# Attention layer on one core: the second attention half writes three of its four head pairs through DRAM, and its products stand behind the transposes

## The chip, the cores and the metric

The kernel runs on one core of a Trainium2 chip. The metric is the device time of one execution in microseconds (us), the median of several runs.

## What is computed

One decoder layer over 1024 tokens plus 16 meta tokens, width 1024. After a norm and a projection come two attentions of 8 heads each, both of head width 64: a stick-breaking attention, and a softmax attention over at most 256 keys that an indexer selects. Their outputs go through branch weights and sigmoid gates, an output weight, and a squared-ReLU MLP. What matters here is the second attention and what it hands on:

```python
logits = jnp.einsum('bqhd,bqkhd->bhqk', qb, kg) * (D_HEAD ** -0.5)
logits = jnp.where(sel_ok[:, None], logits, -jnp.inf)
p = jax.nn.softmax(logits, axis=-1)
return jnp.einsum('bhqk,bqkhd->bqhd', p, vg)
...
merged = gate_sb * (o_sb @ w_branch_sb) + gate_ds * (o_ds @ w_branch_dsa)
```

## The kernel before

Every fp32 factor is split into a rounded "hi" part and a rest, "lo", and a product is made of hi and lo parts on TensorE (PE). The attention is a list of 128 jobs, JOBS, one for each head and block of 128 queries: jobs 0 to 63 are the stick-breaking heads 0 to 7, jobs 64 to 127 the softmax heads 8 to 15. Within a head the blocks come in the order 7, 0, 6, 1, 5, 2, 4, 3; a block i has 16 + 128 (i + 1) keys, in chunks of at most 512. A loop over steps j, written out by hand for each engine, sets all order. In the second half a step does this:

- PE: scores(j) (L759, L760) into two banks in turn; its first part's products (L810); turn(j - 2), the transposes of the weights of two steps ago (L775); at j % 8 == 4 values(), transposes of the next head's values (L741); at PAIR_AT turn_sums(), transposes of the reciprocal sums of a head pair (L785); then its second part's products.
- ScalarE (ACT): round_weights(j - 2), the cast of the turned weights to pt_hi (L932); at j % 8 == 4 the cast of the values (L941); exponent(j) (L916), which waits for VectorE's logits(j); at RELOAD + 3 the cast of a reloaded pair to o_hi (L967); output(k) of a finished product group; at PAIR_AT the cast of a scaled pair (L963).
- VectorE (DVE): logits(j) (L1163), which frees the score banks; rest_weights(j - 2) (L1192), pt_lo = turned weights - pt_hi; add_bottom (L1206); rest_values (L1200); scale_pair (L1181).
- GpSimd (POOL): the add of a reloaded pair (L681), and the rests o_lo (L684, L688).
- SyncE (SP): the DMA queue, strictly in order.

A product group k = 4 g + n belongs to head g and two of its blocks. Its PSUM result has 128 rows, two parts of 64 that still have to be added. In the first half ACT copies it to o_st (L949), SP writes it to DRAM (`spill`, L599), and later SP loads the two parts of a head pair as o_raw0 and o_raw1 (L648), POOL adds them, ACT rounds them. In the second half ACT copies the upper 64 rows to o_pair (L952) and DVE adds the lower 64 from PSUM (L1206). A group of head g ends in steps 8 g + 6, 8 g + 7, 8 g + 10 and 8 g + 11. Four of SP's steps matter below:

```python
for k in OUT_AT[j]:
    if k < 4 * H:
        spill(k)
if j % NB == 1 and j // NB + 1 < 2 * H:
    ...
    load_head(g)
```

load_head issues six loads of q and k and then two of v_raw. The first half's pairs are reloaded at RELOAD = 70, 80, 90, 100; the first half's last spill stands in step 67.

Of the kernel before, what the change touches and what calls it, by code (L numbers as in the profile page):

```python
# [21 lines left out]
D = 1024  # L22
SEQ = 1024
# [251 lines left out]
def build(nc, x, meta, w_units, b_gate, g_pre, g_post, g_mlp_pre, g_mlp_post, ident, strict, fill,  # L275
          rope_i, rope_d, out):
    with ExitStack() as ctx:
# [9 lines left out]
        def scratch(name, *shape):  # L287
            return nc.dram_tensor(name, shape, F32, kind="Internal").ap()
# [4 lines left out]
        def head_rows(d, half, g):  # L293
# [3 lines left out]
            return d[DS][half].rearrange("(d h) t -> h d t", h=H)[g - H]  # L297
        g_d, o_d = scratch("g_d", 2 * D, SEQ), scratch("o_d", H, 2 * DH, SEQ)
        h1_d = nc.dram_tensor("h1_d", (SEQ, D), F32, kind="Internal").ap()
# [191 lines left out]
        with ExitStack() as st:  # L491
# [44 lines left out]
            def _(sp):  # L536
# [86 lines left out]
                for j in range(NJ + 5):  # L623
                    for u in STARTS[j]:
                        load_unit(sp, u + 2, u % 2)
                    for part in range(2):
                        for n in ENDS[j][part]:
                            store(n)
                    for k in OUT_AT[j]:
                        if k < 4 * H:  # L630
                            spill(k)
                    if j % NB == 1 and j // NB + 1 < 2 * H:
                        g = j // NB + 1
                        for u in HEAD_UNITS[g]:
# [3 lines left out]
                    for p in range(4):  # L638
                        if j == RELOAD[p]:
                            for s in range(2):  # L640
                                sp.wait_ge(o_spilled[s], 16 * 4 * (p + 1))
                            if p == 0:
                                in_dram(U_BRANCH - 1)
                            else:
                                sp.wait_ge(or_lo, p)
                            for half in range(2):
                                for g in range(2):
                                    sp.dma_start(o_raw[half][DH * g:DH * g + DH], o_d[2 * p + g, DH * half:DH * half + DH, :]).then_inc(or_in, 16)  # L648

            @block.gpsimd  # L650
            def _(pool):
# [25 lines left out]
                for j in range(NJ // 2 + 1, NJ + 6):  # L677
                    for p in range(4):
                        if j == RELOAD[p] + 1:
                            pool.wait_ge(or_in, 64 * (p + 1))  # L680
                            pool.tensor_tensor(o_raw[0][:], o_raw[0][:], o_raw[1][:], ALU.add).then_inc(or_sum, 1)  # L681
                        if j == RELOAD[p] + 3:
                            pool.wait_ge(or_hi, p + 1)
                            pool.tensor_tensor(o_lo[:, p, :], o_raw[0][:], o_hi[:, p, :].bitcast(F32), ALU.subtract).then_inc(or_lo, 1)  # L684
                    for p in range(3):
                        if j == PAIR_AT[p]:
# [168 lines left out]
            def _(act):  # L855
# [87 lines left out]
                def output(k):  # L943
                    g = k // 4
                    act.wait_ge(pv_done, k + 1)
                    if g < H:
                        if k >= 2:
                            act.wait_ge(o_spilled[k % 2], 16 * (k // 2))
                        act.copy(o_st[:, k % 2], o_part(k)).then_inc(o_free, 1)  # L949
                    else:  # L950
                        r = DH * (g % 2)
                        act.copy(o_pair[(g - H) // 2][r:r + DH, pair_cols(k)], o_part(k)[0:DH]).then_inc(top_done, 1)  # L952

# [10 lines left out]

                def reload(p):
                    act.wait_ge(or_sum, p + 1)
                    act.copy(o_hi[:, p, :], o_raw[0][:]).then_inc(or_hi, 1)  # L967
# [7 lines left out]
                for j in range(NJ + 5):  # L975
# [12 lines left out]
                    for n in ENDS[j][1]:  # L988
                        evacuate(n)
                    for p in range(4):  # L990
                        if j == RELOAD[p] + 3:
                            reload(p)
                    if j > NJ // 2 and j % 16 == 0:
# [3 lines left out]
                    for p in range(3):  # L997
                        if j == PAIR_AT[p]:
                            round_pair(p)

            @block.vector
            def _(dve):
# [168 lines left out]
                def scale_pair(p):  # L1171
                    if p < 3:
                        dve.wait_ge(o_free, 4 * H + 8 * (p + 1))
                    else:
                        dve.wait_ge(or_lo, 4)
                    for half in range(2):
# [25 lines left out]
                def add_bottom(k):  # L1202
                    g, r = k // 4, DH * (k // 4 % 2)
                    dst = o_pair[(g - H) // 2][r:r + DH, pair_cols(k)]
                    dve.wait_ge(top_done, k + 1 - 4 * H)
                    dve.tensor_tensor(dst, dst, o_part(k)[DH:P], ALU.add).then_inc(o_free, 1)  # L1206
# [18 lines left out]
                for j in range(NJ + 6):  # L1225
                    if 1 <= j < NJ + 1 and JOBS[j - 1][0] == SB:
                        stick(j - 1)
                    if j > NJ // 2 and j % 16 == 0:
                        reciprocals((j - NJ // 2) // 16 - 1)
                    if j < NJ and JOBS[j][0] == DS:  # L1230
                        logits(j)
# [4 lines left out]
                    while spent < due:  # L1236
                        spent += next(search, 1e9)
                    if 2 <= j < NJ + 2:
# [4 lines left out]
                    if j % NB == 4 and j // NB + 1 < 2 * H:  # L1243
                        rest_values(j // NB + 1)
                    if j in PAIR_AT:
                        scale_pair(PAIR_AT.index(j))
                    if j < NJ + 5:
# [1004 lines left out]
```

## Time and profile before

| | us |
|---|---|
| median of 3 runs | 1745.53 |
| the three runs | 1745.53, 1737.97, 1750.38 |
| profiled execution, its time | 1746.8 |
| its span, first to last instruction | 1745.0 |
| second attention half within it | 723.2 to 918.3 |
| mean granted TensorE clock | 0.972 of full speed |

Busy shares of the whole span: PE 94%, weight loads 79%, DVE 71%, ACT 49%, POOL 31%. PE's busy time counts matmuls from start to modelled end, which overlap, so it is an upper bound of its work. A time is a place in the span, counted from its start. A head in the second half is told here by the start of ACT's exponent over 1040 keys, the head's first job: 728.11, 752.15, 773.09, 798.40, 819.45, 844.36, 865.30 and 888.11 for heads 8 to 15.

### The profile page before, as it was taken

To read this page: it belongs to the slowest core of one execution; us is meant where nothing else is said; L and a number is where in the kernel's file an instruction comes from. 1 tells how busy PE (TensorE), PEld (TensorE's weight loads), DVE (VectorE), ACT (ScalarE), POOL (GpSimd) and SP (SyncE) were. 2 spreads that over 40 slices of the span, in tenths; PEclk is the share of its full clock that TensorE was granted. 3 is DMA by queue.
4 is the path that set the end of the run, shared out by engine and by line. 5 is a ranking of instruction groups with operands and counts; after the bars stand their busy time and mean duration, and the time that the engine had idled before them with its cause. 6 is when DMAs were issued, how large, how long until landed. Compare 5 with 4: busy or idle time off the path is not lost. (4 is left out here: it accounts for less than half of the span.)

```text
span 1745.0 us, 23454 instructions
## 1 busy us (share of the span) xinstructions
PE 1638.4 (94%) x8360; PEld 1384.4 (79%) x8360; DVE 1245.4 (71%) x1966; ACT 851.5 (49%) x1650; POOL 539.7 (31%) x332
## 2 busy tenths in 40 slices
PE   4999899999999999889889999989999999999997
PEld 4889888799877777777777878768888878888885
DVE  5287798888988989687873435785454548777878
ACT  5266555555445545576751133555555543333334
POOL 1111254555434435321102450475545510000000
PEclk6999999999999999998989999999999999999999
DMA  4564434344233233355304443243444365443434
GB/s 172 155 194 124 128 120 134 108 137 114 89 106 107 92 106 107 91 134 135 86 1 163 139 169 121 72 158 133 145 149 174 136 229 217 157 159 131 169 138 103
DMA packets 101372, 231.23 MB, mean 133 GB/s; under 512 B 11192, under 2 KB 25848, under 8 KB 101256
## 3 DMA queue, kind: packets, MB, share of 16 engines
q1 hardware_dynamic: 100680, 227.64, 40.7%
q0 software_dynamic: 576, 2.10, 0.7%
q8 instruction: 67, 1.10, 0.3%
q14 instruction: 49, 0.40, 0.1%
HBM read 155.83 MB, written 73.86 MB: 132 GB/s over the span
## 5 line engine op out<-in xcount | busy, mean ns | idle before, releaser
L710 PE MATMUL bk<-x_hi,w_hi 128*128 128x512 f32 (+2 forms) x832 | 308.7, 371 | 1.2 <-PEq L353 1.2
L710 PE MATMUL bk<-x_lo,w_hi 128*128 128x512 f32 (+2 forms) x832 | 299.3, 360 | 0.0
L710 PE MATMUL bk<-x_hi,w_lo 128*128 128x512 f32 (+2 forms) x832 | 298.5, 359 | 0.0
L666 POOL TENSOR_TENSOR pt_lo<-a_buf,pt_hi 128x512 fp32r<-128x512 f32 (+3 forms) x104 | 138.4, 1347 | 193.0 <-ACT pt_hi L930 192.8
L334 POOL TENSOR_TENSOR w_lo<-w_raw,w_hi 128x1024 fp32r<-128x1024 f32 x53 | 130.4, 2460 | 190.9 <-ACT w_hi L330 190.7
L1087 DVE TENSOR_SCALAR_CACHE_REDUCE counted<-sc,small 128x272 uint8<-128x272 f32 (+6 forms) x217 | 182.5, 891 | 0.9
L1674 PE MATMUL bank<-v_hi,f_hi 128*128 128x512 f32 x448 | 174.3, 389 | 0.0
L1674 PE MATMUL bank<-v_hi,f_lo 128*128 128x512 f32 x448 | 174.3, 389 | 0.0
L1674 PE MATMUL bank<-v_lo,f_hi 128*128 128x512 f32 x448 | 174.3, 389 | 0.0
L710 PEld LDWEIGHTS bk<-x_hi,w_lo 128*128 128x128 f32 x832 | 158.5, 191 | 17.6
L710 PEld LDWEIGHTS bk<-x_hi,w_hi 128*128 128x128 f32 x832 | 159.1, 191 | 16.1 <-issue 1.3
L710 PEld LDWEIGHTS bk<-x_lo,w_hi 128*128 128x128 f32 x832 | 158.8, 191 | 13.3
L810 PE MATMUL bk<-pt_hi,v_hl 128*128 128x256 f32 (+2 forms) x384 | 115.2, 323 | 10.6 <-ACT o_st L949 5.7
L1542 POOL TENSOR_TENSOR s_lo<-s,s_hi 128x512 fp32r<-128x512 f32 x64 | 95.2, 1491 | 72.9 <-ACT s_hi L1718 72.9
L1192 DVE TENSOR_TENSOR pt_lo<-bk,pt_hi 128x512 fp32r<-128x512 f32 (+2 forms) x120 | 62.4, 553 | 74.3 <-ACT pt_hi L932 73.0
L929 ACT COPY a_buf<-bk 128x512 f32<-128x512 f32 (+3 forms) x104 | 54.3, 522 | 107.4 <-PE bk L775 107.4
L1542 POOL TENSOR_TENSOR s_lo<-u_raw,s_hi 128x512 fp32r<-128x512 f32 x48 | 67.9, 1419 | 123.9 <-ACT s_hi L1718 123.9
L775 PE MATMUL bk<-idf,a_buf 128*128 128x128 f32 (+1 forms) x704 | 101.0, 278 | 4.1 <-DVE pt_lo L1192 2.5
L1143 DVE TENSOR_TENSOR_SCAN n_buf<-n_buf 128x1040 f32<-128x1040 f32 (+3 forms) x64 | 101.9, 1591 | 2.3 <-ACT n_buf L906 2.3
L810 PEld LDWEIGHTS bk<-pt_hi,v_hl 128*128 128x128 f32 (+1 forms) x384 | 76.9, 200 | 32.4 <-issue 14.6
L759 PE MATMUL bk<-k_hi,q_st 128*128 128x348 f32 (+6 forms) x224 | 80.1, 361 | 22.9 <-ACT n_buf L906 11.6
L1651 PE MATMUL bank<-m_hi,s_hi 128*128 128x512 f32 x256 | 99.9, 390 | 1.1 <-DVE m_lo L1939 1.1
(228 smaller groups left out, 3861.0 us busy)
## 6 DMA issues: line engine op xcount, KB each, us to landing
w_raw<-w_units SPq DMA_DIRECT2D x57, 512.0 KB, 3.7
f_raw<-f_d SPq DMA_DIRECT2D x28, 1024.0 KB, 5.0
u_raw<-w_units SPq DMA_DIRECT2D x32, 512.0 KB, 4.8
f_d<-f_s SPq DMA_DIRECT2D x64, 256.0 KB, 2.2
b<-w_units SPq DMA_DIRECT2D x16, 1024.0 KB, 8.3
f_d<-c SPq DMA_DIRECT2D x48, 256.0 KB, 2.1
k_hi<-k_d SPq DMA_DIRECT2D x32, 260.0 KB, 5.6
k_lo<-k_d SPq DMA_DIRECT2D x32, 260.0 KB, 6.1
```

Source lines behind the costliest of these rows:

```text
L334: pool.tensor_tensor(w_lo[:, s], w_raw[:, s], w_hi[:, s].bitcast(F32), ALU.subtract).then_inc(lo_done, 1)
L666: pool.tensor_tensor(pt_of(pt_lo, j, tiles), raw, pt_of(pt_hi, j, tiles).bitcast(F32), ALU.subtract).then_inc(sb_lo, 1)
L710: mm = pe.matmul(pj[b][:, 0:c1 - c0], w[:, s, kt, :], a[:, kt, c0:c1], start=kt == 0 and k == 0, stop=kt == KT - 1 and k == 2)
L759: pe.matmul(dst, q, k_hi[s][:, c0:c1], start=True, stop=False)
L775: mm = pe.transpose(bk[TP_BANK[n]][0:r, m * P:(m + 1) * P], a_buf[:, j % 3, col:col + r], idf[:])
L810: mm = pe.matmul(dst, v_hl[0:r, g % 2, slot, :], w[0:r, cols], start=slot == 0 and w is hi, stop=slot == o + 1 and w is lo)
L1087: op(dve.tensor_scalar(counted[:, blk(b)], sc[:, blk(b)], cand[:, j:j + 1], None, ALU.is_ge, ALU.add, accum_out=cnt[:, j:j + 1]))
L1143: dve.tensor_tensor_scan(n[:, ::-1], n[:, ::-1], n[:, ::-1], 1.0, ALU.mult, ALU.bypass).then_inc(scan_done, 1)
L1192: dve.tensor_tensor(pt_of(pt_lo, j, tiles), bk[TP_BANK[n]][:, 0:m * P].rearrange("p (c k) -> p c k", c=m), pt_of(pt_hi, j, tiles).bitcast( ...
L1542: pool.tensor_tensor(s_lo[k % RING][:], first_raw(*FIRST[k]), s_hi[k % RING][:].bitcast(F32), ALU.subtract).then_inc(s_lo_done, 1)
L1651: mm = pe.matmul(dst, w[r][:, n, :], b, start=p in (1, 2, 5) and n == 0 and i == 0, stop=n == HT - 1 and i == 2, skip_group_check=True)
L1674: mm = pe.matmul(dst, a[r][:, q, t * P:(t + 1) * P], w[r][:, q, :], start=p in (1, 5, 2) and q == 0 and n == 0, stop=q == QP - 1 and n == ...
```

## The change

The second half's three first head pairs (heads 8 to 13, groups 32 to 55) are treated as the first half's: ACT copies all 128 rows to o_st, SP spills them, and three more reloads bring them back, the one part into o_pair, the other into o_raw1; POOL adds them and DVE's scale_pair waits for that. Only heads 14 and 15 keep the old way. The seven reloads stand at steps 70, 78, 85, 90, 95, 101 and 117. From step 66 PE runs all products of a step behind the transposes. DVE's rest_weights moves from the end of a step to the start of the next, and rest_values and scale_pair one step on; PAIR_AT moves four steps on.

```diff
+SECOND_HALF = NJ // 2 + 2
-RELOAD = [NJ // 2 + 6 + 10 * p_ for p_ in range(4)]
-PAIR_AT = [NJ // 2 + 16 * (p_ + 1) + 4 for p_ in range(3)] + [NJ + 1]
+RELOAD = [(NJ // 2 + step_, p_) for step_, p_ in ((6, 0), (14, 1), (21, 4), (26, 2), (31, 3), (37, 5), (53, 6))]
+PAIR_AT = [NJ // 2 + 16 * (p_ + 1) + 8 for p_ in range(3)] + [NJ + 1]
+K_LAST = 4 * H + 24
@@ SP
-                        if k < 4 * H:
+                        if k < K_LAST:
                             spill(k)
-                        if j == RELOAD[p]:
+                        if j == step:
                             for s in range(2):
                                 sp.wait_ge(o_spilled[s], 16 * 4 * (p + 1))
-                            if p == 0:
+                            if n == 0:
                                 in_dram(U_BRANCH - 1)
                             else:
+                                sp.wait_ge(or_sum, n)
+                            if 1 <= p < 4:
                                 sp.wait_ge(or_lo, p)
@@ POOL
+                        if j == step + 1:
+                            whole = o_raw[0] if p < 4 else o_pair[p - 4]
+                            pool.wait_ge(or_in, 64 * (n + 1))
+                            pool.tensor_tensor(whole[:], whole[:], o_raw[1][:], ALU.add).then_inc(or_sum, 1)
@@ PE
-                    for k, slots in PRODUCTS[j][0]:
-                        product(k, slots)
+                    if j < SECOND_HALF:
+                        for k, slots in PRODUCTS[j][0]:
+                            product(k, slots)
...
+                    if j >= SECOND_HALF:
+                        for k, slots in PRODUCTS[j][0]:
+                            product(k, slots)
@@ ACT
-                    if g < H:
+                    if k < K_LAST:
                         if k >= 2:
                             act.wait_ge(o_spilled[k % 2], 16 * (k // 2))
                         act.copy(o_st[:, k % 2], o_part(k)).then_inc(o_free, 1)
...
-                        if j == RELOAD[p] + 3:
-                            reload(p)
+                        if j == step + 3 and p < 4:
+                            reload(n, p)
@@ DVE
+                    if j > SECOND_HALF and j - 3 < NJ:
+                        rest_weights(j - 3)
...
-                        if k >= 4 * H:
+                        if k >= K_LAST:
                             add_bottom(k)
```

PE in a step whose first part has products (the third step of head 15; pt_hi and pt_lo are the weights, a_buf what is turned), before:

```order
L759 MATMUL bk<-k_hi_352,q_st_350 128x456 [waits f_zdused]
L760 MATMUL bk<-k_lo_354,q_st_350 128x456
L759 MATMUL bk<-k_hi_352,q_st_350 128x456 [waits f_zdused]
L760 MATMUL bk<-k_lo_354,q_st_350 128x456
L810 MATMUL bk<-pt_hi_359,v_hl 128x256 [waits f_tpfree]
L810 MATMUL bk<-pt_lo_361,v_hl 128x256
```

and the same place in the change:

```order
L764 MATMUL bk<-k_hi_352,q_st_350 128x456 [waits f_zdused]
L765 MATMUL bk<-k_lo_354,q_st_350 128x456
L764 MATMUL bk<-k_hi_352,q_st_350 128x456 [waits f_zdused]
L765 MATMUL bk<-k_lo_354,q_st_350 128x456
L780 MATMUL bk<-idf,a_buf 16x128 [waits f_tpfree,f_exp]
L780 MATMUL bk<-idf,a_buf 128x128 x3
L780 MATMUL bk<-idf,a_buf 128x128 [waits f_tpfree]
L780 MATMUL bk<-idf,a_buf 128x128 x3
L780 MATMUL bk<-idf,a_buf 128x128 [waits f_tpfree]
L815 MATMUL bk<-pt_hi_359,v_hl 128x256 [waits f_tpfree]
L815 MATMUL bk<-pt_lo_361,v_hl 128x256
```

The transposes (L775, now L780) moved ahead of the products (L810, now L815).

SP around the third reload of a first-half pair (step 90), before: the loads of head 12 and at once the reload.

```order
L594 DMA v_raw<-v_d 64x528
L595 DMA v_raw<-v_d 64x512
L648 DMA o_raw_347<-o_d 64x1024 [waits f_orlo,f_ospill1,f_ospill0]
L648 DMA o_raw_347<-o_d 64x1024
```

In the change:

```order
L601 DMA o_d<-o_st 128x256 [waits f_ofree] x2
L593 DMA q_st_349<-q_d 64x1024 [waits f_stored0,f_stored1,f_z,f_tp]
L594 DMA k_hi_351<-k_d 64x1040
L595 DMA k_lo_353<-k_d 64x1040
L593 DMA q_st_349<-q_d 64x1024
L594 DMA k_hi_351<-k_d 64x1040
L595 DMA k_lo_353<-k_d 64x1040
L596 DMA v_raw<-v_d 64x528
L597 DMA v_raw<-v_d 64x512
L601 DMA o_d<-o_st 128x256 [waits f_ofree]
L652 DMA o_raw_347<-o_d 64x1024 [waits f_orsum,f_orlo,f_ospill1,f_ospill0]
```

Spills now stand ahead of the head's loads and between them and the reload, and each waits for ACT's copy of that step (f_ofree).

DVE where a head begins (L1163, now L1172, are logits; 128x144 is the head's second job), before:

```order
L1192 TENSOR_TENSOR pt_lo_361<-bk,pt_hi_359 128x4x128 [waits f_tphi]
L1192 TENSOR_TENSOR pt_lo_361<-bk,pt_hi_359 128x2x128 [waits f_tphi]
L1206 TENSOR_TENSOR o_pair_366<-o_pair_366,bk 64x256 [waits f_top]
L1163 ISA n_buf,small<-bk,small 128x144 [waits f_z,f_exp]
L1163 ISA small 128x1
```

and in the change:

```order
L1202 TENSOR_TENSOR pt_lo_361<-bk,pt_hi_359 128x4x128 [waits f_tphi]
L1202 TENSOR_TENSOR pt_lo_361<-bk,pt_hi_359 128x2x128 [waits f_tphi]
L1172 ISA n_buf,small<-bk,small 128x144 [waits f_z,f_exp]
L1172 ISA small 128x1
```

Only the add left; rests and logits stand in the order in which they stood.

## Rows read from the trace of the kernel before

**Rows 1.** Windows of the second half, and heads 9, 10, 13, 14.

```profile
core 0: us, PE busy (x) PEld busy (x) DVE busy (x) ACT busy (x) POOL busy (x), PEclk, DMA share, GB/s
723.20:918.30 195.10, 166.19 (x1088) 140.45 (x1087) 141.93 (x394) 130.91 (x311) 32.06 (x16) 0.91 0.41 93
752.15:773.09 20.94, 18.03 (x131) 15.07 (x129) 17.31 (x50) 15.36 (x38) 4.77 (x2) 1.00 0.64 143
773.09:798.40 25.31, 21.90 (x139) 18.55 (x137) 18.39 (x51) 17.15 (x41) 4.74 (x2) 0.87 0.32 71
844.36:865.30 20.94, 18.04 (x131) 15.07 (x129) 17.29 (x50) 14.39 (x38) 0.51 (x1) 1.00 0.43 93
865.30:888.11 22.81, 19.31 (x136) 16.21 (x135) 18.21 (x51) 16.16 (x39) 2.38 (x1) 0.97 0.18 38
```

**Rows 2.** Waits in head 13: total us, times, longest.

```profile
ACT pt_hi L932 <- PE bk L775: 5.1, 4, 2.0
DVE pt_lo L1192 <- ACT pt_hi L932: 2.5, 5, 1.0
...
PE bk L759 <- DVE small L1163: 1.5, 1, 1.5
...
PE bk L775 <- DVE pt_lo L1192: 0.8, 1, 0.8
PE bk L810 <- issue: 0.5, 1, 0.5
```

**Rows 3.** Timeline of head 13, third step: last product, turn, cast, rest.

```profile
847.60 0.28 PE L810 MATMUL bk<-pt_lo,v_hl 128*128 128x128 f32 x1
...
847.72 1.15 PE L775 MATMUL bk<-idf,a_buf 128*16 128x128 f32 x9
...
848.97 0.69 DVE L1192 TENSOR_TENSOR pt_lo<-bk,pt_hi 128x512 fp32r<-128x512 f32 x1 [0.52 <-ACT pt_hi L932]
```

**Rows 4.** Timeline of head 13, seventh step: first product, turn, rest.

```profile
857.01 0.28 PE L810 MATMUL bk<-pt_hi,v_hl 128*128 128x256 f32 x1
...
857.90 0.93 PE L775 MATMUL bk<-idf,a_buf 128*16 128x128 f32 x7
...
859.15 0.69 DVE L1192 TENSOR_TENSOR pt_lo<-bk,pt_hi 128x512 fp32r<-128x512 f32 x1 [1.01 <-ACT pt_hi L932]
```

**Rows 5.** DVE's adds, by line, from 720 to 925.

```profile
L1206 DVE TENSOR_TENSOR o_pair<-o_pair,bk 64x256 f32<-64x256 f32 x32 | 13.6, 424 | 5.8 <-ACT o_pair L952 4.9
```

**Rows 6.** Timeline: one spill; head 14's loads, ACT's output before them, values() in head 13.

```profile
724.72 0.32 SPq L599 DMA_DIRECT2D o_d<-o_st  x1
...
838.83 0.44 SPq L591 DMA_DIRECT2D q_st<-q_d  x1
...
842.32 0.36 ACT L952 COPY o_pair<-bk 64x256 f32<-64x256 f32 x1
...
842.51 0.60 SPq L594 DMA_DIRECT2D v_raw<-v_d  x1
843.15 0.60 SPq L595 DMA_DIRECT2D v_raw<-v_d  x1
...
852.37 0.53 PE L741 MATMUL bk<-idf,v_raw 64*16 64x64 f32 x9
```

**Rows 7.** DMA issues from 720 to 920: KB each, median us to landing.

```profile
v_raw<-v_d SPq DMA_DIRECT2D x7, 128.0 KB, 6.4
```

**Rows 8.** Timeline: a reload that nothing else overlaps, and POOL's add of it.

```profile
757.96 2.36 SPq L648 DMA_DIRECT2D o_raw<-o_d  x4
...
765.05 2.39 POOL L681 TENSOR_TENSOR o_raw<-o_raw,o_raw 128x1024 f32<-128x1024 f32 x1 [7.19 <-DMA o_raw<-o_d]
```

**Rows 9.** ACT: output and, three steps on, the cast's place, for steps 70, 78, 90.

```profile
747.38 0.36 ACT L952 COPY o_pair<-bk 64x256 f32<-64x256 f32 x1
...
754.34 1.06 ACT L967 CAST o_hi<-o_raw 128x1024 fp32r<-128x1024 f32 x1
...
768.18 0.36 ACT L952 COPY o_pair<-bk 64x256 f32<-64x256 f32 x1
...
775.82 0.44 ACT L916 ACTIVATE a_buf<-n_buf,small 128x144 f32<-128x144 f32 x1
...
804.57 0.36 ACT L952 COPY o_pair<-bk 64x256 f32<-64x256 f32 x1
...
811.26 1.03 ACT L967 CAST o_hi<-o_raw 128x1024 fp32r<-128x1024 f32 x1
```

**Rows 10.** Window with the granted clock in head 10.

```profile
786.00:790.00 4.00, 4.00 (x17) 3.54 (x16) 1.77 (x5) 2.04 (x4) 2.37 (x1) 0.50 0.02 4
```

More of the change, by code:

```diff
@@ L637, in _ @@
                         load_head(g)
-                    for p in range(4):
-                        if j == RELOAD[p]:
+                    for n, (step, p) in enumerate(RELOAD):
+                        if j == step:
                             for s in range(2):
                                 sp.wait_ge(o_spilled[s], 16 * 4 * (p + 1))
-                            if p == 0:
+                            if n == 0:
                                 in_dram(U_BRANCH - 1)
                             else:
+                                sp.wait_ge(or_sum, n)
+                            if 1 <= p < 4:
                                 sp.wait_ge(or_lo, p)
-                            for half in range(2):
+                            for half, dst in enumerate((o_raw[0] if p < 4 else o_pair[p - 4], o_raw[1])):
                                 for g in range(2):
-                                    sp.dma_start(o_raw[half][DH * g:DH * g + DH], o_d[2 * p + g, DH * half:DH * half + DH, :]).then_inc(or_in, 16)
+                                    sp.dma_start(dst[DH * g:DH * g + DH], o_d[2 * p + g, DH * half:DH * half + DH, :]).then_inc(or_in, 16)
             @block.gpsimd
@@ L677, in _ @@
                 for j in range(NJ // 2 + 1, NJ + 6):
[L678 to L681, printed above, removed]
-                        if j == RELOAD[p] + 3:
+                    for n, (step, p) in enumerate(RELOAD):
+                        if j == step + 1:
[3 more added lines that the diff above has]
+                        if j == step + 3 and p < 4:
                             pool.wait_ge(or_hi, p + 1)
@@ L951, in output @@
                         r = DH * (g % 2)
-                        act.copy(o_pair[(g - H) // 2][r:r + DH, pair_cols(k)], o_part(k)[0:DH]).then_inc(top_done, 1)
+                        act.copy(o_pair[3][r:r + DH, pair_cols(k)], o_part(k)[0:DH]).then_inc(top_done, 1)
                 def spread(p):
@@ L963, in round_pair, with reload @@
                     act.copy(o_hi[:, 4 + p, :], o_pair[p][:]).then_inc(op_hi, 1)
-                def reload(p):
-                    act.wait_ge(or_sum, p + 1)
+                def reload(n, p):
+                    act.wait_ge(or_sum, n + 1)
                     act.copy(o_hi[:, p, :], o_raw[0][:]).then_inc(or_hi, 1)
@@ L989, in _ @@
                         evacuate(n)
-                    for p in range(4):
-                        if j == RELOAD[p] + 3:
-                            reload(p)
+                    for n, (step, p) in enumerate(RELOAD):
+                        if j == step + 3 and p < 4:
+                            reload(n, p)
                     if j > NJ // 2 and j % 16 == 0:
@@ L1172, in scale_pair @@
                     if p < 3:
-                        dve.wait_ge(o_free, 4 * H + 8 * (p + 1))
+                        dve.wait_ge(or_sum, [q for _, q in RELOAD].index(4 + p) + 1)
                     else:
+                        dve.wait_ge(or_sum, len(RELOAD))
                         dve.wait_ge(or_lo, 4)
@@ L1237, in _ @@
                         spent += next(search, 1e9)
-                    if 2 <= j < NJ + 2:
+                    if 2 <= j < SECOND_HALF:
                         rest_weights(j - 2)
                     for k in (OUT_AT[j - 1] if j else ()):
-                        if k >= 4 * H:
+                        if k >= K_LAST:
                             add_bottom(k)
[L1243 to L1246, printed above, removed]
+                    late = int(j > SECOND_HALF)
+                    if (j - late) % NB == 4 and (j - late) // NB + 1 < 2 * H:
+                        rest_values((j - late) // NB + 1)
+                    if j - late in PAIR_AT:
+                        scale_pair(PAIR_AT.index(j - late))
                     if j < NJ + 5:
```

12 lines of the change are left out of this document (6 added, 6 removed).

## The prediction

> **What bounds the kernel now.** I read the windows first. The second attention half takes 195.1 us of the 1745.0 [rows 1]; nothing outside it is touched, so all that follows is a sum over its eight heads. An undisturbed head (9 or 13) takes 20.94 us at full clock, and in it PE is busy 18.0 us, DVE 17.3 and ACT 14.4 to 15.4 [rows 1]. So three engines are nearly full at once, PE most of all. PE idles 2.9 us in such a head, and the waits say where [rows 2]: 1.5 us once, when the third chunk of the head's first scores waits for DVE's logits; 0.8 us once, when a transpose waits for a bank that DVE's rest has to free; 0.5 us once ahead of a product. No change of order alone can give more than these 2.9 us a head. DVE itself waits 2.5 us for ACT's casts, and ACT 5.1 us for PE's transposes [rows 2]: the ring PE transpose, ACT cast, DVE rest, DVE logits, PE scores goes around, and products stand inside it.
>
> Heads 10 and 14, in which a pair's sums are turned and scaled, take 25.31 and 22.81 us [rows 1]. The second is nearly all at full clock (0.97) and so shows the price of the pair, 22.8 - 20.9 = 1.9 us. The first ran at 0.87; its extra 2.5 us is the price of one stretch at half clock, 1.2 GHz [rows 10]. The mean clock of the half is 0.91 [rows 1].
>
> **The change part by part: what it gives.** (a) DVE loses 24 of the 32 adds at 0.424 us [rows 5], 10.2 us of work, four adds (1.7 us) in each of six heads; ACT's copy of 128 rows in place of 64 has the same columns and I cost it at nothing. (b) On PE the transposes go ahead of the products of the first part. In the third step of head 13 DVE waits 0.52 us for the cast behind the transpose at 847.72, which starts when the products end [rows 3]; in the seventh step the products take 857.90 - 857.01 = 0.9 us and DVE waits 1.01 us behind them [rows 4]. Both waits go. (c) DVE's rests change their place in the code but not in its sequence, so that edit alone is worth nothing.
>
> What does PE get of this? Between the seventh step and the next head's scores DVE wins the wait of 1.0, one add of 0.4 and some 0.2 of smaller gaps: 1.6 us, and the scores' wait of 1.5 us is covered by it. The product's 0.5 shrinks to 0.3 with it. The bank's 0.8 stays, since between step 2 and step 5 PE, ACT and DVE are all packed and products only change places with transposes. That is 1.7 us a head for heads 8 to 13. In heads 14 and 15 the adds remain and I take 1.0. Sum 6 x 1.7 + 2 x 1.0 = 12.2 us. (d) turn_sums leaves the step in which it shares four banks with two groups of weights and two of values. PE's eight transposes and DVE's two multiplies remain. I take half of the 1.9 us, 0.9 for each of three pairs: 2.8. Together 15 us are given.
>
> **What it costs.** (e) The spills tie SP to ACT. Until now SP ran ahead in this half: head 14's loads were issued from 838.83, and v_raw's two loads at 842.51 and 843.15 [rows 6], landing 6.4 us after issue [rows 7], at 849.6, well ahead of values() at 852.37. Now the spill of the head's last step stands ahead of load_head and waits for ACT's output, which ended at 842.32 + 0.36 = 842.68. With 0.3 for the spill's issue the loads start at 843.0, v_raw's second follows 843.15 - 838.83 = 4.3 later, and lands at 843.0 + 4.3 + 6.4 = 853.7. That is 1.3 us too late at the old pace, and 2.0 with the quicker head. PE already waits 0.8 us right behind (the bank), so some 1.2 are left. Six heads (9 to 14) are concerned; in 9, 10 and 12 the next item comes before it and hides it. 3 x 1.2, less what head 11 shares with its reload: 3 us.
>
> (f) The reloads. A reload is issued at step j, and ACT takes its sum at step j + 3, whatever SP did. Before, SP ran ahead and ACT never waited. Now reloads 70, 78, 90 and 95 stand directly behind a spill of the same step, so behind ACT's output of that step. From there: 0.3 for the spill's issue [rows 6], 765.05 - 757.96 = 7.1 from the first issue to landing, and 2.4 for POOL's add [rows 8]: the sum is there 9.8 us after the output ended. ACT reaches its cast after 754.34 - 747.74 = 6.6 us (step 70), 776.26 - 768.54 = 7.7 (step 78), 811.26 - 804.93 = 6.3 (step 90) [rows 9]. ACT would stand 3.2, 2.1 and 3.5 us. For step 95, which is followed by a head's long first jobs but whose reload also waits for POOL's previous rest, I estimate 1.5 (between 0 and 3.5, the ends of the others). Behind the waiting ACT stand the casts of the next weights; DVE waits for them with its next logits, and PE can run ahead only by two score banks. Lower bound of the cost: nothing, if ACT, 73% busy, catches up. Upper: all of it. After each of these places ACT, PE and DVE are packed for four steps (there ACT has no slack to give), so I take all: 10.3 us.
>
> For (f) the Trainium skill says otherwise: "DMA: Bandwidth & Descriptors", section "Anatomy of one DMA — SWDGE (gpsimd) path", fits a DMA as 2.0 us plus its bytes at 436 GB/s. Taken for the 1 MB of a reload as a whole, my estimate by that page is 4.4 us; ACT's stands would shrink to some 0.5, 0, 0.8 and 0, and the kernel would come out near 1736. The row of this trace has 7.1 us with POOL idle and waiting for it, for DMAs of SP's queue, so the sum goes by the row.
>
> (g) Three more reloads (85, 101, 117) feed DVE's scale_pair. From the last spill of a pair to that step lie six steps, some 15 us at 2.6 a step; the way is 0.3, the spill's landing (which I take at 2, between nothing and v_raw's 6.4), 7.1 and 2.4, some 12 us and at most 16.2. Covered, or nearly. POOL's adds, 7 us, are hidden: it is busy 4.8 of 21 us in a head [rows 1].
>
> Sum: 3 + 10.3 = 13.3 us of cost against 15.0 given, so 1.7 less: 1746.8 - 1.7 = 1745.1. The profiled execution is 1.3 above the median of the runs, which is inside their spread of 12 us. **Forecast: 1745 us**, no change that can be told; about 1% (17 us) is what a measurement of this kernel can tell from none.
>
> **The rivals.** *The stands are hidden.* If ACT's waits fall into idle time (it waits 5.1 us a head for PE anyway [rows 2]) or the reloads land sooner, only (e) is left: -15 + 3 = -12. A denser PE may also lose one or two of the half-clock stretches at 2.5 each: -14.5 to -17, so 1730 to 1735. For it: DVE, not ACT, is the engine PE waits for. Against it: in the packed steps every cast is followed at once by someone's wait. Chance 0.27. Of it 0.05 is for the shorter transfer by the fit of the Trainium skill.
>
> *The stands bring half clock, and it is slower.* Place: the four waits of ACT and three of v_raw. A stand of 2 to 3.5 us leaves PE without work, longer than the 1.5 us that it waits now. If five of seven stands open one more stretch at 2.5 us, that is 12.5; with all of (e) and (f) at the quicker pace (0.6 more on each of the seven, 4) the sum is -15 + 13.3 + 4 + 12.5 = +15: 1762. It decides from about three extra stretches. For it: the clock fell in head 10 (0.87) with no stand at all. Against it: head 13 has its wait of 1.5 us and stayed at 1.00 [rows 1, 2]. Chance 0.18.
>
> *The order does nothing.* PE is at 18 of 20.9 us, and products behind transposes may delay the next scores by what the transposes gain. Then 5 us are given, and at the slower pace the costs are 9: 1751. Chance 0.07.
>
> The forecast itself, 1738 to 1752, has 0.48.
>
> **How the numbers follow.** The range leaves out half of the best end of the first rival and the upper half of the second: 1730 to 1760. Faster by over 1% (under 1729) needs the first rival and both clock gains: 0.14. Slower by over 1% (over 1763) is the far half of the second: 0.12. The rest, 0.74, is within.
>
> **What would show it.** In the changed profile: an undisturbed head (13 after the change) 19 to 20.5 us; no wait of L759's successor for logits over 0.5 us; ACT's cast of o_hi from o_raw waiting for POOL's add three or four times, 1.5 to 4 us each (this is the step I am least sure of); PE's transposes of v_raw waiting for a DMA, 1 to 2 us, in three to six heads; scale_pair not waiting for POOL; the mean clock of the half near 0.91. If those waits of ACT are absent, (f) is wrong and the time lies near 1733; if they are there and the heads are still short, ACT had the slack that I deny it.

## The result: slower by 1.0%, and the profile after

| | before | after |
|---|---|---|
| median of 4 runs each | 1741.97 us | 1759.67 us |
| lowest and highest | 1737.97, 1750.38 | 1756.43, 1764.86 |
| profiled execution: time, span | 1746.8, 1745.0 | 1758.25, 1756.1 |
| second half in it | 723.2 to 918.3 | 724.3 to 930.9 |

The ratio is 1.0104, with the interval 1.0059 to 1.0149: 17.7 us slower. The second run of the changed kernel, inside the experiments below, gave 1.0092 [1.0070, 1.0114]. The profiled executions are 11.5 us apart in time, and 11.5 us lie in the second half: 206.6 us in place of 195.1. That is less than 17.7 because runs of one kernel spread by 8 to 12 us, and the profiled execution of before was a long one, 4.8 us above its median, while that of the change lies 1.4 below its own. Waits and places can be compared between the two profiles; a difference of a few us in total time or a few hundredths of mean clock can't.

The windows of the changed kernel, for the half and for heads 9, 10, 12, 13 and 14, and one stretch in head 12:

```profile
core 0: us, PE busy (x) PEld busy (x) DVE busy (x) ACT busy (x) POOL busy (x), PEclk, DMA share, GB/s
724.30:930.90 206.60, 171.19 (x1088) 143.04 (x1086) 129.85 (x370) 129.31 (x311) 39.12 (x19) 0.89 0.50 118
754.51:780.09 25.58, 20.00 (x128) 16.68 (x127) 15.54 (x46) 15.08 (x39) 4.73 (x2) 0.90 0.66 150
780.09:802.28 22.19, 19.24 (x134) 15.93 (x133) 15.12 (x45) 15.91 (x39) 7.09 (x3) 0.96 0.75 172
828.67:856.15 27.48, 22.72 (x134) 19.05 (x133) 15.03 (x45) 15.92 (x39) 7.11 (x3) 0.80 0.63 147
856.15:878.62 22.47, 19.32 (x136) 16.15 (x135) 16.52 (x48) 15.07 (x38) 2.38 (x1) 0.97 0.48 114
878.62:901.79 23.17, 21.06 (x134) 17.39 (x134) 15.78 (x46) 14.87 (x39) 2.36 (x1) 0.88 0.56 131
842.00:850.00 8.00, 8.00 (x35) 7.04 (x33) 2.85 (x9) 2.73 (x7) 1.01 (x1) 0.50 0.54 131
```

Beside [rows 1], DVE has lost its 24 adds (394 to 370 instructions, 141.93 to 129.85 us busy) and POOL has gained 7 us, both as meant. Still none of heads 8 to 14 is shorter than before's undisturbed 20.94. Head 9 grew by 4.6 us. Heads 10 and 14, which no longer turn a pair's sums (that is now in heads 11, 13 and 15), take 22.19 and 23.17 us. The last row is a stretch of 8 us at half clock within head 12. Head 12 was not free of half clock before: it ran at 0.50 from 820.00 to 825.00, at its start. Its mean clock was 0.89, as this row of before shows, and is 0.80 now:

```profile
819.45:844.36 24.91, 21.68 (x142) 18.39 (x140) 18.39 (x51) 17.11 (x41) 6.59 (x3) 0.89 0.51 114
```

The waits from 720 to 960, the same columns as [rows 2], of which these rows matter:

```profile
DVE pt_lo L1202 <- ACT pt_hi L941: 46.0, 38, 4.9
...
ACT pt_hi L941 <- PE bk L815: 36.1, 14, 5.6
...
PE bk L764 <- DVE small L1172: 18.3, 22, 4.0
...
ACT pt_hi L941 <- PE bk L780: 15.2, 12, 2.9
...
ACT o_hi L976 <- POOL o_raw L686: 10.8, 3, 4.9
...
PE bk L746 <- DMA v_raw<-v_d: 6.6, 4, 3.8
...
DVE small L1178 <- ACT a_buf L925: 3.1, 4, 0.9
```

The same view of before, over the same stretch:

```profile
ACT pt_hi L932 <- PE bk L775: 43.3, 32, 3.9
...
DVE pt_lo L1192 <- ACT pt_hi L932: 29.1, 39, 3.2
...
PE bk L759 <- DVE small L1163: 11.1, 9, 1.6
...
ACT o_hi L963 <- DVE o_pair L1181: 6.8, 3, 2.5
```

Four of the rows shown are new after the change: ACT's cast of the weights waits for products (L815), ACT's o_hi for POOL, PE for v_raw, DVE's reciprocal for ACT. The first is the largest, and the prediction doesn't name it. Its 36.1 us are not a loss of 36.1: the cast's wait for transposes fell from 43.3 to 15.2 at the same time, so ACT's waits for PE before this cast grew by 8.0 in all. What such a row costs is read from the times of the experiments. DVE's wait for the casts grew by 16.9 us, PE's wait for logits by 7.2. One wait went: ACT no longer stands for DVE's scaled pair (6.8 us).

Where that first wait is from shows in the timeline of head 13. Its third step, which answers to [rows 3]:

```profile
859.58 1.14 PE L780 MATMUL bk<-idf,a_buf 128*16 128x128 f32 x9
...
860.48 0.36 PE L815 MATMUL bk<-pt_hi,v_hl 128*128 128x256 f32 x1
...
861.10 0.28 PE L815 MATMUL bk<-pt_lo,v_hl 128*128 128x128 f32 x1
...
861.46 1.07 ACT L941 CAST pt_hi<-bk 128x512 fp32r<-128x512 f32 x2 [1.87 <-PE bk L815]
...
862.08 0.69 DVE L1202 TENSOR_TENSOR pt_lo<-bk,pt_hi 128x512 fp32r<-128x512 f32 x1 [1.12 <-ACT pt_hi L941]
```

And its seventh, which answers to [rows 4]:

```profile
869.76 0.93 PE L780 MATMUL bk<-idf,a_buf 128*16 128x128 f32 x7
...
870.44 0.36 PE L815 MATMUL bk<-pt_hi,v_hl 128*128 128x256 f32 x1
...
871.66 0.97 ACT L941 CAST pt_hi<-bk 128x512 fp32r<-128x512 f32 x2 [2.21 <-PE bk L815]
...
872.28 0.69 DVE L1202 TENSOR_TENSOR pt_lo<-bk,pt_hi 128x512 fp32r<-128x512 f32 x1 [1.29 <-ACT pt_hi L941]
```

The transposes start ahead of the products, as planned, but the cast behind them starts 1.9 us after they do, and only when the last product has ended. pt_hi and pt_lo have two buffers, one for each product group in turn, and round_weights holds one more wait:

```python
if k == 0 and pair_of(j) >= 2:
    act.wait_ge(pv_done, pair_of(j) - 1)
```

The weights turned in the third and the seventh step go into the buffer from which the products of that same step read. While the products stood first, that wait was met when the transposes ended: in the waits of before, the cast waits for L775 only, never for L810. Now transposes and products run one after the other before the cast may start. DVE's waits of 0.52 us [rows 3] and 1.01 us [rows 4] became 1.12 and 1.29.

The reload of step 70 in the timeline, and the casts of the next and of the fifth reload:

```profile
750.54 0.37 ACT L958 COPY o_st<-bk 128x256 f32<-128x256 f32 x1
...
750.94 0.32 SPq L601 DMA_DIRECT2D o_d<-o_st  x1
...
751.42 2.37 SPq L652 DMA_DIRECT2D o_raw<-o_d  x4
...
758.76 2.37 POOL L686 TENSOR_TENSOR o_raw<-o_raw,o_raw 128x1024 f32<-128x1024 f32 x1 [25.60 <-DMA o_raw<-o_d]
...
761.16 1.05 ACT L976 CAST o_hi<-o_raw 128x1024 fp32r<-128x1024 f32 x1 [4.34 <-POOL o_raw L686]
...
784.92 1.05 ACT L976 CAST o_hi<-o_raw 128x1024 fp32r<-128x1024 f32 x1 [1.57 <-POOL o_raw L686]
...
820.20 1.04 ACT L976 CAST o_hi<-o_raw 128x1024 fp32r<-128x1024 f32 x1 [4.89 <-POOL o_raw L686]
...
821.77 1.16 DVE L1202 TENSOR_TENSOR pt_lo<-bk,pt_hi 128x512 fp32r<-128x512 f32 x2 [4.92 <-ACT pt_hi L941]
```

From the end of ACT's output (750.91) to the sum (761.13) it is 10.2 us. ACT stands, and in the last two rows DVE stands just as long behind it. The values' loads, in heads 12 and 13:

```profile
841.37 0.76 PE L746 MATMUL bk<-idf,v_raw 64*16 64x64 f32 x9 [3.78 <-DMA v_raw<-v_d]
...
854.04 0.35 ACT L958 COPY o_st<-bk 128x256 f32<-128x256 f32 x1
...
854.41 0.33 SPq L601 DMA_DIRECT2D o_d<-o_st  x1
...
855.39 0.45 SPq L593 DMA_DIRECT2D q_st<-q_d  x1
...
859.73 0.59 SPq L597 DMA_DIRECT2D v_raw<-v_d  x1
```

Head 14's loads start 0.8 us before head 13 does (856.15); before, they started 5.5 us before it (838.83 and 844.36). SP waits for ACT. The longest wait, 3.78 us in head 12, is for loads that stood behind the fifth reload as well, and PE's 8 us at half clock follow it directly. These loads also took 7.8 to 8.2 us to land, where the median in this half is 6.5.

### The profile page after: what moved, and what is told of

Read it like the earlier page. It is cut to its first block and busy times, and to the rows that moved or that the text cites. A ratio compares the mean times of both kernels' runs of the same rounds, so it can differ in the third digit from the quotient of the medians.

```text
span 1756.1 us, 23499 instructions
## 1 busy us (share of the span) xinstructions
PE 1644.8 (94%) x8360; PEld 1388.2 (79%) x8360; DVE 1230.6 (70%) x1942; ACT 850.0 (48%) x1650; POOL 550.0 (31%) x335
## 5 line engine op out<-in xcount | busy, mean ns | idle before, releaser
L815 PE MATMUL bk<-pt_hi,v_hl 128*128 128x256 f32 (+2 forms) x384 | 115.0, 323 | 9.6 <-ACT o_st L958 6.1
L780 PE MATMUL bk<-idf,a_buf 128*128 128x128 f32 (+1 forms) x704 | 105.7, 287 | 3.2 <-DVE pt_lo L1202 1.6
L1572 POOL DMA_DIRECT2D out<-scaled x4 | 3.6, 897 | 314.8 <-DVE scaled L2150 314.8
```

The lines of the kernel that those rows point to most:

```text
L780: mm = pe.transpose(bk[TP_BANK[n]][0:r, m * P:(m + 1) * P], a_buf[:, j % 3, col:col + r], idf[:])
L815: mm = pe.matmul(dst, v_hl[0:r, g % 2, slot, :], w[0:r, cols], start=slot == 0 and w is hi, stop=slot == o + 1 and w is lo)
```

## Experiments

Ratios are to the kernel before, run beside it on the same chip, with 95% intervals; 1% is 17.4 us. A ratio uses all runs, so it can differ from the quotient of the two medians by up to 0.001. Prices in us are worked out from the ratios. Where two changed kernels are compared, both intervals count: a difference under some 0.003, 5 us, is not clear of noise.

**The order alone.** The kernel before, with only PE's order of the change:

```diff
-                    for k, slots in PRODUCTS[j][0]:
-                        product(k, slots)
+                    if j < NJ // 2 + 2:
+                        for k, slots in PRODUCTS[j][0]:
+                            product(k, slots)
...
+                    if j >= NJ // 2 + 2:
+                        for k, slots in PRODUCTS[j][0]:
+                            product(k, slots)
                     for k, slots in PRODUCTS[j][1]:
```

> The kernel before with only PE's order changed: from step 66 the products of the first part stand behind the transposes. Theory (the cast waits for the products): 4 to 8 us slower than before, 1.002 to 1.005, with ACT's cast waiting some 30 us in all for products, and DVE's wait in the third step of a head 1.1 in place of 0.5 us. Rival 1 (the order is neutral): within 1 us of before. Rival 2 (the order gives what the prediction took, about 1 us a head): 6 to 10 us faster.

Measured: 1747.95 us, 1.0035 [1.0021, 1.0049], so 6.1 us slower. Its waits, and its head 13 in the third step:

```profile
ACT pt_hi L936 <- PE bk L810: 29.1, 20, 2.8
```

```profile
849.11 1.25 ACT L936 CAST pt_hi<-bk 128x512 fp32r<-128x512 f32 x3 [2.27 <-PE bk L810]
...
849.73 1.49 DVE L1196 TENSOR_TENSOR pt_lo<-bk,pt_hi 128x512 fp32r<-128x512 f32 x3 [1.12 <-ACT pt_hi L936]
```

With nothing spilled, the wait for products is there, in the place and with the DVE wait of 1.12 us that the changed kernel has. The order costs; it doesn't give. The cast's waits for PE add up to 43.0 us here (29.1 for products, 13.9 for transposes) against 43.3 before, so the 6.1 us come not from a longer sum of waits but from where they stand.

**The order undone.** The changed kernel with the products first again:

```diff
-                    if j < SECOND_HALF:
-                        for k, slots in PRODUCTS[j][0]:
-                            product(k, slots)
+                    for k, slots in PRODUCTS[j][0]:
+                        product(k, slots)
...
-                    if j >= SECOND_HALF:
-                        for k, slots in PRODUCTS[j][0]:
-                            product(k, slots)
```

> The changed kernel with PE's order undone: products of the first part ahead of the transposes again, all else as changed. Theory (the order itself costs, since ACT's cast may not overwrite pt_hi before the products of the same step have read it, so with products last the cast waits for transposes and products one after the other): the wait of ACT's cast for products (36 us in all) goes, a head gets 0.6 to 1.2 us shorter, the kernel 5 to 9 us faster than the changed one, 1.005 to 1.008 of the kernel before; the stands of ACT for the reloads and of PE for v_raw stay or grow. Rival (the order is neutral or gives something, all of the loss is stands): no faster than the changed kernel, 1.009 to 1.013.

Measured: 1748.85 us, 1.0048 [1.0029, 1.0066]. That is 8 to 10 us better than the change (1.0092 and 1.0104), a little more than the 5 to 9 expected. ACT's waits for POOL (10.8 us) and PE's for v_raw (8.5 us) stay.

**The casts later.** The changed kernel, ACT's cast of a reloaded pair and POOL's rest of it at the reload's step + 5 in place of + 3:

```diff
-                        if j == step + 3 and p < 4:
+                        if j == step + 5 and p < 4:
```

> The changed kernel with ACT's cast and POOL's rest of a reloaded pair five steps behind the issue in place of three. Theory (ACT's stands of 4.3, 1.6 and 4.9 us cost in full): ACT no longer waits for POOL's add, 8 to 10 us faster than the changed kernel, less 2 us since the reload of step 95 must wait longer for POOL: 1.004 to 1.007 of before. Rival (ACT had the slack): at most 3 us faster than the changed kernel, 1.009 to 1.011.

Measured: 1759.39 us, 1.0109 [1.0093, 1.0124]: no gain at all, and the expectation missed. ACT's stand for POOL is gone, but two other waits grew from 36.1 and 6.6 us:

```profile
ACT pt_hi L941 <- PE bk L815: 47.0, 17, 5.3
...
PE bk L746 <- DMA v_raw<-v_d: 12.9, 5, 7.1
```

The waits for v_raw have two origins. In head 9 (first row of the changed kernel, second of this run) the loads were issued at the same place in both, but while ACT stood 4.34 us, v_raw had time to land; without that stand PE arrives earlier and waits:

```profile
767.34 0.76 PE L746 MATMUL bk<-idf,v_raw 64*16 64x64 f32 x9
...
767.00 0.76 PE L746 MATMUL bk<-idf,v_raw 64*16 64x64 f32 x9 [3.89 <-DMA v_raw<-v_d]
```

In head 12 the wait grew from 3.78 to 7.12 us, and there PE does not arrive earlier: it starts to wait at 837.42, against 837.59 in the changed kernel. The values land later, since the edit itself delays SP. The fifth reload must wait until POOL's rest of the pair before it is done (`or_lo`), and that rest now stands two steps later. The reload moves from 825.54 to 828.22, and head 13's loads stand behind it:

```profile
825.54 2.56 SPq L652 DMA_DIRECT2D o_raw<-o_d  x4
...
SPq L649 <- POOL o_lo L689: 1.8, 1, 1.8
...
828.22 2.37 SPq L652 DMA_DIRECT2D o_raw<-o_d  x4
...
844.54 0.76 PE L746 MATMUL bk<-idf,v_raw 64*16 64x64 f32 x9 [7.12 <-DMA v_raw<-v_d]
```

So this run doesn't price ACT's stands alone. The kernels below that cast later also move the fifth reload behind head 13's loads.

**The values first.** The changed kernel, the two loads of v_raw ahead of the six of q and k:

```diff
@@ load_head
+                    sp.dma_start(v_raw[0:DH, :], v_d[g * DH:(g + 1) * DH, 0:T // 2 + 8]).then_inc(v_in, 16)
+                    sp.dma_start(v_raw[DH:P, 0:T // 2 - 8], v_d[g * DH:(g + 1) * DH, T // 2 + 8:T]).then_inc(v_in, 16)
...
-                    sp.dma_start(v_raw[0:DH, :], v_d[g * DH:(g + 1) * DH, 0:T // 2 + 8]).then_inc(v_in, 16)
-                    sp.dma_start(v_raw[DH:P, 0:T // 2 - 8], v_d[g * DH:(g + 1) * DH, T // 2 + 8:T]).then_inc(v_in, 16)
```

> The changed kernel with load_head's two loads of v_raw ahead of the six of q and k. Theory (PE's four waits for v_raw, 6.6 us in all, cost most of their length): the waits go, 4 to 6 us faster than the changed kernel, 1.006 to 1.009 of before. Rival (PE gets the time back as the ring of DVE and ACT is what is late): within 2 us of the changed kernel, 1.009 to 1.012.

Measured: 1749.20 us, 1.0048 [1.0031, 1.0066]. The waits for v_raw are gone. The gain is 8 to 10 us, where 4 to 6 were expected and the waits add up to 6.6; the intervals leave some 5 us on either side, so that it is more than their length is likely and not shown.

**All three.** Products first, casts at + 5 with the fifth reload two steps later (at 33 for 31), values first:

> The changed kernel with three edits together: products ahead of the transposes again, the casts of the reloaded pairs five steps behind the issue (and the fifth reload at step 97, behind the loads of head 13, in place of 95), v_raw loaded first. What is left of the change is the way through DRAM. Theory (order, stands of ACT and stands for v_raw are all of the loss, and what is saved on DVE is worth something once they are gone): no wait for v_raw, none of ACT for POOL, faster than before by 3 to 10 us, 0.994 to 0.998. Rival (PE and its half-clock stretches set the time, DVE's adds are worth nothing): 0.999 to 1.001.

Measured: 1737.89 us, 0.9973 [0.9956, 0.9989]. The way through DRAM can pay. Not every stand is gone: ACT waits once, 2.4 us, for POOL's add of a reloaded pair, and DVE and ACT now wait for the moved pairs (below).

**The same with the order of the change**, so that the order is priced where no stand hides it:

> The same as the kernel with all three edits, but with the change's order on PE (products behind the transposes). Theory (both stands gone, the order's 6 us remain): 1.000 to 1.003, 5 to 8 us behind the kernel with all three. In the run with the cast alone moved, the stand only changed its place from ACT to PE's wait for v_raw (12.9 us); here neither is left. Rival (the cast is useless also with v_raw first): 1.004 to 1.006, as with v_raw first alone.

Measured: 1745.79 us, 1.0022 [1.0004, 1.0039]. Against the kernel just above, run beside it, the order costs 0.0049, 8.5 us, clear of noise.

**The casts kept.** Products and values first, the casts left at + 3 and the fifth reload at 31:

> The changed kernel with products ahead of the transposes again and v_raw first, but ACT's casts of the reloaded pairs left three steps behind the issue. Against the kernel with all three edits (0.9973) it prices ACT's stands alone, where no later wait for v_raw can take their place. Theory (the stands, some 11 us in three places, cost most of their length): ACT waits 10 to 11 us for POOL's add, 1.001 to 1.004 of before, 6 to 11 us slower than with all three edits. Rival (ACT has the slack, as the run with the cast alone moved could be read): 0.997 to 0.999.

Measured: 1742.63 us, 1.0011 [1.0000, 1.0021], 0.0038 or 6.6 us behind the kernel with all three. Its stands for POOL:

```profile
ACT o_hi L972 <- POOL o_raw L686: 11.1, 3, 5.5
```

The kernel with all three has 2.4 us of these, so 8.7 us fewer, and in turn 3.9 us of DVE's waits for POOL, which this one lacks. The 6.6 us are the price of the early casts and the earlier fifth reload together; the stands cost a good part of their length, and how much exactly stays open.

**SP tied to ACT, no transfers.** The kernel before, where SP waits at the places of the 24 new spills, but moves nothing:

```diff
                         if k < 4 * H:
                             spill(k)
+                        elif k < 4 * H + 24:
+                            sp.wait_ge(top_done, k + 1 - 4 * H)
```

> The kernel before, its way of the second half kept, with nothing but a wait in SP where the change has a spill: for each of groups 32 to 55 SP waits for ACT's copy of that group. Theory (the tie of SP to ACT costs, not the transfers): ACT stands some 3 us before its casts in steps 73 and 93, PE waits 1 to 2 us for v_raw in three to five heads, 1.003 to 1.007. Rival (the added transfers or their landing cost, the tie does not): 0.999 to 1.001.

Measured: 1752.32 us, 1.0063 [1.0040, 1.0086], 11 us slower, with both kinds of new wait:

```profile
ACT o_hi L969 <- POOL o_raw L683: 5.5, 2, 3.1
...
PE bk L743 <- DMA v_raw<-v_d: 3.2, 3, 2.0
```

Stands of both kinds thus come from the tie alone, with none of the new traffic there. They are smaller than in the changed kernel (10.8 and 6.6 us); of the four reloads, which stand at steps 70, 80, 90 and 100 here, only those at 70 and 90 share their step with the end of a group. What makes up the rest in the changed kernel, the later and denser reloads or the transfers, was not separated.

**DVE's adds left out.** The kernel before without the adds of groups 32 to 55. The lower part of heads 8 to 13 is not added in; ACT's copy then frees the bank:

```diff
-                        act.copy(o_pair[...][r:r + DH, pair_cols(k)], o_part(k)[0:DH]).then_inc(top_done, 1)
+                        act.copy(o_pair[...][r:r + DH, pair_cols(k)], o_part(k)[0:DH]).then_inc(o_free if k < 4 * H + 24 else top_done, 1)
...
-                        if k >= 4 * H:
+                        if k >= 4 * H + 24:
                             add_bottom(k)
```

> The kernel before without DVE's adds of groups 32 to 55: the lower 64 rows of heads 8 to 13 are left out of the result, nothing else changes. It prices term (a) of the prediction alone, 10.2 us of DVE's work. Theory (DVE stands in the ring with PE, some 0.5 us a head come out): 3 to 6 us faster, 0.997 to 0.998. The prediction's own figure for heads without adds, with the order: 1.7 us a head, 0.994. Rival (PE sets the time): 0.999 to 1.001.

Measured: 1729.21 us, 0.9931 [0.9911, 0.9951], 12.0 us faster for 10.2 us of DVE's work, where 3 to 6 were expected: a miss. The edit also lets ACT's copy free the bank in place of DVE's add, as the change does; before has no wait of PE for an add in this half. Windows of the half and of head 13:

```profile
core 0: us, PE busy (x) PEld busy (x) DVE busy (x) ACT busy (x) POOL busy (x), PEclk, DMA share, GB/s
723.20:901.22 178.02, 154.93 (x1089) 131.42 (x1088) 129.43 (x371) 130.98 (x311) 32.07 (x16) 0.97 0.44 101
835.11:854.67 19.56, 17.81 (x131) 15.07 (x129) 15.27 (x46) 14.31 (x37) 1.14 (x1) 1.00 0.44 97
```

An undisturbed head takes 19.56 us against 20.94 [rows 1], 1.4 less for 1.7 of adds, with both at full clock; over six heads that is 8.3 us. The half's mean clock is 0.97 against 0.91, but these profiled executions lie 2.6 us below the median (this run) and 5.7 above it (before), so the pair overstates the difference. Over all runs the mean clock of the whole program is 0.986 without the adds (6 runs) and 0.980 before (23 runs): the same direction, and smaller.

**The reciprocals.** The kernel with all three, and DVE's reciprocals of a pair's sums behind rest_weights again, where they stood before the change:

```diff
-                    if j > NJ // 2 and j % 16 == 0:
-                        reciprocals((j - NJ // 2) // 16 - 1)
...
+                    if j > NJ // 2 and j % 16 == 0:
+                        reciprocals((j - NJ // 2) // 16 - 1)
```

> The kernel with all three edits, and DVE's reciprocals of a pair behind the step's rest of the weights in place of ahead of it, as in the kernel before. Theory (ahead of the rests DVE waits 0.9 us for ACT's exponent, 3.1 us in four places, and PE's scores wait for DVE there): the wait goes, 1 to 3 us faster than with all three edits, 0.995 to 0.997 of before. Rival (the wait only takes the place of another): the same as with all three edits, 0.997.

Measured: 1732.50 us, 0.9954 [0.9931, 0.9978]: 8.0 us faster than the kernel before with the whole computation, and the fastest such kernel here. DVE's wait for the exponent is gone. Against the kernel with all three it is 3.3 us faster (0.9973 and 0.9954, each against its own runs of before); the intervals overlap, so this step is not clear of noise.

**The pair's sums later still.** That kernel with PAIR_AT + 11 for + 8:

> The same, and the sums of a pair turned and scaled three steps later still (steps 91, 107 and 123 in place of 88, 104 and 120), so that the pair's reload has three steps more to arrive. Theory (DVE's waits of 3.9 us in two places for POOL's add of a reloaded pair, longest 2.9, cost their length): these waits go, 2 to 4 us faster than the one without this edit, 0.993 to 0.996 of before. Rival (the pair's work costs the same wherever it stands): no difference, 0.995 to 0.997.

Measured: 1738.69 us, 0.9974 [0.9958, 0.9989]. By 3.5 us slower than the kernel above, where I expected faster; the two intervals overlap, so at least the gain of 2 to 4 us isn't there. DVE's waits for POOL's add are gone as meant, but its waits for ACT's casts rose from 27.7 to 32.4 us.

**The change again**, word for word, beside the two kernels above:

> The changed kernel once more, word for word, on the same chip as the two beside it, to set the steps between the kernels against one another: 1.009 to 1.012 of before, by both theories.

Measured: 1757.19 us, 1.0092 [1.0070, 1.0114].

## Why the prediction was wrong

The forecast was 1745, no change; 17.7 us were lost. The measured 1759.67 lies just inside the range of 1730 to 1760 only because the sum started from the profiled 1746.8, 4.8 above the median of before. In differences, 1.7 us of gain were predicted and 17.7 us of loss came. The experiments form a chain from before to after: the adds left out, -12.0; the adds done through DRAM and POOL, with the pairs moved and everything spaced well, +4.0 (0.9954 against 0.9931); the reciprocals moved, +3.3 (0.9973 against 0.9954); the order, +8.5; the values' loads last, the casts early and the fifth reload two steps sooner, +12 to +14 (1.0022 to 1.0092 or 1.0104). The sum is +16 to +18, and must be, since each link starts where the last one ends; the +4.0 and the +3.3 are not clear of noise, the others are.

Beside the prediction's sum this says where it went wrong. The costs (e) and (f), put at 13.3 together, measured 12 to 14. The gains, put at 15.0, measured a loss of about 4: 12.0 from the adds, less 8.5 for the order, 3.3 for the reciprocals and 4.0 for the way through DRAM with the moved pairs.

**The step that failed is (b)**, "on PE the transposes go ahead of the products", with its "Both waits go". They became longer, since ACT's cast of those weights needs the buffer that the products still read. The part of the 12.2 us that was to come from it, some 8 us, came out as a cost of 6.1 us alone and of 8 to 10 in the changed kernel. That the releaser is the buffer is read from the traces and the code; a third pair of buffers, which would prove it, was not tried.

(a), DVE's adds, gave all that (a) and (b) together were to give: 12.0 us measured, 12.2 predicted. That the two numbers agree is luck. In the prediction, 1.0 of the 1.7 us a head is (b)'s wait, and of four adds one counts. So the order was to bring 8 us (8 x 1.0) and the adds some 4 (6 x 0.7); measured are a loss of 6.1 to 8.5 and a gain of 12.0. Beside it less of the half ran at half clock. If all the rest of it ran at full clock, that time is twice (1 - mean clock) times the length: 0.09 x 195.1 x 2 = 35 us before, 0.03 x 178.0 x 2 = 11 us without the adds, and 0.11 x 206.6 x 2 = 45 us after the change. These are single executions. Outside the half, where the kernels do the same, they differ as well: the whole program has 0.028 x 1745 x 2 = 98 us at half clock before and 0.024 x 1756 x 2 = 84 after, which leaves 63 and 39 us outside the half. The mean over the runs moves the same way for the change, 0.976 (6 runs) against 0.983 (19 runs of before beside them).

(c), "worth nothing", was wrong in one piece. The rests kept their sequence, but the reciprocals came to stand ahead of them and wait for ACT's exponent: four waits of up to 0.9 us, 3.1 in all. Moving them back brought 3.3, which is not clear of noise.

(d), the pair's move, was not tried alone. ACT's wait of 6.8 us for the scaled pair is gone, which speaks for a gain; that three steps further gave nothing, and measured 3.5 us slower, says that later isn't simply better. The 2.8 us are not shown. Naming head 13 as undisturbed was a slip: its first step now turns a pair's sums.

(e), SP tied to ACT, was right as a mechanism and too small: 3 us predicted, 6.6 us of waits in four places measured, worth 8 to 10. It placed them wrongly too: of heads 9, 10 and 12, which it called hidden, 10 and 12 had 1.41 and 3.78 us, and heads 11 and 13 only 0.57 and 0.84. I took each wait alone and left out that in head 12 the loads stand behind a spill and a late reload at once.

(f), the stands of ACT, was right in mechanism and length: 3.2, 2.1, 3.5 and 1.5 us predicted, 4.34, 1.57, 4.89 and none measured (10.3 against 10.8), and 10.2 us to the sum against 9.8. They were to cost all of their length; 6.6 us came back when the casts and the fifth reload were moved with the values already early. Moved alone, the casts gave nothing, in head 9 because PE then waits for the values, in head 12 because the fifth reload comes later. The 4.4 us for a reload that I had worked out from "DMA: Bandwidth & Descriptors" of the Trainium skill were not borne out: 758.76 - 751.42 = 7.3 us. The section, "Anatomy of one DMA — SWDGE (gpsimd) path", has its fit for one DMA issued from GpSimd; these are four of 256 KB from SP's queue.

(g) held: DVE never waited for POOL's sum in the changed kernel. In the quicker kernel with all three edits it does, 3.9 us in two places:

```profile
DVE o_pair L1187 <- POOL o_pair L686: 3.9, 2, 2.9
```

Of the rivals, the one of half clock behind the stands came nearest (1762), and part of its mechanism is seen: after 3.78 us of wait PE ran 8 us at 0.50. But its sum started from a gain of 15 us that the order was to give in part, and the order gave none. That the order does nothing was a rival at 1751, by a delay of the next scores and not of the cast; that it costs was not among them. What stays open is how much of each price is the wait itself and how much the clock, and what in the 4.0 us is the way through DRAM and what the moved pairs.

## What to carry to other kernels

Before a consumer is moved behind the producer of the next item, list every wait of the engine that overwrites a buffer, not only the waits for data: with two buffers the reader that was moved may hold the one wanted next. A spill put into an in-order DMA queue ties all later loads to the engine that fills it, even where nothing is transferred (11 us here); put the loads with the nearest deadline first and give each reload's consumer some steps of distance. An edit that takes away one wait may measure as nothing (1.0109 here) and still be worth 6.6 us in better company, for two reasons that only the trace tells apart: the next wait was hidden behind the first (head 9), or the edit itself delays another queue (head 12, where a later rest on POOL held a reload and all loads behind it). So look where each new wait comes from, try fixes together, and then take them out one by one.

## What was unexpected of the hardware

Taking 10.2 us of work from DVE, which was busy 73% of the half, gave 12.0 us. An undisturbed head at full clock gave 1.4 us for 1.7 of adds, 8.3 over six heads, so the rest has another source; the mean granted clock of TensorE is higher without the adds, 0.986 against 0.980 over the runs, which would fit. The other way round, small waits may cost more than their length: taking away 6.6 us of PE's waits for v_raw gave 8 to 10, with some 5 us of uncertainty, and the longest of them, 3.78 us, is followed by 8 us at 0.50. No run here isolates the clock from the rest.
